# Matmul operands moved: activation rows 320 columns apart, operands at multiples of 512 bytes, a smaller scratch for DMAs

## What is computed

```
mod = silu(c) @ w_ada + b_ada                      # 2048 -> 6 * 2048, per sequence
h   = rmsnorm(x, norm1_g) * (1 + scale1) + shift1
qa, ka, va, qb, kb, vb, r, glr = split(h @ w_in)   # 2048 -> 6160
oa  = dilated window attention(qa, ka, va)         # samples also read 1024 cached rows each
ob  = gated linear attention(qb, kb, vb, gate(glr))
x   = x + gate1 * (concat(norm(oa), norm(ob) * silu(r)) @ w_out)        # 2048 -> 2048
h2  = rmsnorm(x, norm2_g) * (1 + scale2) + shift2
g, u = split(h2 @ w_up)                            # 2048 -> 2 * 5632
x   = x + gate2 * ((silu(causal_conv3(g)) * u) @ w_down)                # 5632 -> 2048
```

## The kernel before

| tensor | start before | above a multiple of 512 | start after | above a multiple of 512 |
|---|---|---|---|---|
| `ring` | 16512 | 128 | 8320 | 128 |
| `v_parts` | 26752 | 128 | 18560 | 128 |
| `kdm` | 126080 | 128 | 117888 | 128 |
| `ghi` | 153568 | 480 | 145376 | 480 |
| `hhi` | 159712 | 480 | 151552 | 0 |
| `hlo` | 178144 | 480 | 172032 | 0 |
| `whi` | 196576 | 480 | 192512 | 0 |
| `wlo` | 212960 | 480 | 208896 | 0 |
| `vals` | 159712 | 480 | 151552 | 0 |
| `kcT` | 200672 | 480 | 192512 | 0 |

## Time and profile before

### The profile page before, as it was taken

One profiled execution on the slowest core, in us unless ns is written; L12 is line 12 of the kernel. 1 busy time (PEld: TensorE's weight loads), 2 busy tenths in 40 slices (PEclk: granted clock), 3 DMA queues, 4 the chain that ended last, 5 costly groups with the idle time before them and its releaser, 6 DMA issues.

```text
span 1667.9 us, 29469 instructions
## 1 busy us (share of the span) xinstructions
PE 1624.7 (97%) x12258; PEld 1457.8 (87%) x12258; DVE 891.6 (53%) x1562; ACT 719.6 (43%) x1026; POOL 75.5 (5%) x132
## 2 busy tenths in 40 slices
PE   8999999999999889999999999999999999999997
PEld 4778888888888545998999999999999999999996
DVE  3555555455665453645654554545545465656563
ACT  3332444444555434534443333333334345545552
POOL 2000000000111000000000000000000000000000
PEclk8999999999999999999999999999999999999998
DMA  9998777778878999765845445554455446555450
GB/s 335 375 376 312 256 248 246 268 266 274 281 263 274 333 378 331 242 227 178 285 148 163 153 155 178 169 162 154 158 178 173 154 137 191 164 173 177 152 188 15
DMA packets 276113, 370.71 MB, mean 222 GB/s; under 512 B 8273, under 2 KB 192947, under 8 KB 275977
## 3 DMA queue, kind: packets, MB, share of 16 engines
q1 hardware_dynamic: 232928, 279.88, 50.6%
q10 hardware_dynamic: 35970, 71.45, 12.1%
q0 software_dynamic: 7088, 17.54, 3.2%
HBM read 358.96 MB, written 9.88 MB: 221 GB/s over the span
## 4 chain that ended last, share of the span: by engine, by line
PE 84%; issue 5%; DVE 4%; DMA 3%; ACT 2%; SPq 1%; POOL 0%; ACTq 0%; DVEq 0%; POOLq 0%
PE ps L920 23%; PE ps L921 22%; PE ps L922 22%; PE ps L871 4%; PE ps L1167 2%; DMA ring<-in_w_in 1%; PE ps L1182 1%; DMA vals<-in_w_ada 1%; PE ps L1212 1%; SPq L524 1%; DMA proj<-in_w_ada 1%; PE ps L878 1%; DVE wlo L1994 1%; ACT whi L1469 0%; PE ps L865 0%
## 5 line engine op out<-in xcount | busy, mean ns | idle before, releaser
L920 PE MATMUL ps<-hhi,whi 128*128 128x288 f32 x3136 | 939.8, 300 | 1.4 <-DVE hlo L1986 0.7
L922 PE MATMUL ps<-hhi,wlo 128*128 128x288 f32 x3136 | 924.5, 295 | 0.0
L921 PE MATMUL ps<-hlo,whi 128*128 128x288 f32 x3136 | 924.1, 295 | 0.0
L920 PEld LDWEIGHTS ps<-hhi,whi 128*128 128x128 f32 x3136 | 588.8, 188 | 40.0 <-issue 34.2
L921 PEld LDWEIGHTS ps<-hlo,whi 128*128 128x128 f32 x3136 | 588.4, 188 | 0.9
L922 PEld LDWEIGHTS ps<-hhi,wlo 128*128 128x128 f32 x3136 | 588.8, 188 | 0.0
L1855 DVE TENSOR_TENSOR wlo<-ring,whi 128x1024 fp32r<-128x1024 f32 x178 | 212.2, 1222 | 88.0 <-ACT whi L1452 87.5
L1452 ACT ACTIVATE whi<-ring 128x1024 fp32r<-128x1024 f32 x178 | 184.6, 1057 | 159.2 <-PE ps L922 159.2
L1994 DVE TENSOR_TENSOR wlo<-ring,whi 128x1024 fp32r<-128x1024 f32 x96 | 117.3, 1224 | 124.3 <-ACT whi L1469 124.1
L1469 ACT ACTIVATE whi<-ring 128x1024 fp32r<-128x1024 f32 x96 | 100.9, 1053 | 139.0 <-PE ps L922 113.9
L2483 DVE TENSOR_TENSOR wlo<-ring,whi 128x1024 fp32r<-128x1024 f32 (+1 forms) x94 | 105.7, 1131 | 57.3 <-ACT whi L1777 57.3
(11 more groups left out here) (312 smaller groups left out, 1189.2 us busy)
## 6 DMA issues: line engine op xcount, KB each, us to landing
ring<-in_w_up SPq DMA_DIRECT2D x88, 1024.0 KB, 5.1
ring<-in_w_ada ACTq DMA_DIRECT2D x58, 1024.0 KB, 8.5
ring<-in_w_in SPq DMA_DIRECT2D x48, 1024.0 KB, 9.1
ring<-in_w_down SPq DMA_DIRECT2D x32, 1408.0 KB, 6.7
ring<-in_cache_k_win SPq DMA_DIRECT2D x16, 1024.0 KB, 9.6
vals<-in_cache_v_win SPq DMA_DIRECT2D x32, 512.0 KB, 8.0
ring<-in_w_out SPq DMA_DIRECT2D x16, 1024.0 KB, 5.9
proj<-in_w_ada SPq DMA_DIRECT2D x14, 1024.0 KB, 10.7
```

The costliest lines, as they stand in the source:

```text
L920: mm(out, w_hi, x_hi, start=start, stop=False)
L921: mm(out, w_hi, x_lo, start=False, stop=False)
L922: return mm(out, w_lo, x_hi, start=False, stop=stop)
```

## The change

Three edits. The rows of `hhi` and `hlo` are put 320 columns apart (1280 bytes), of which the first 288 are used; every slice that the program takes of them is unchanged. `ln_first`, a small tensor that lay behind all others, moves ahead of `hhi` and is 8 columns wide (32 bytes), which shifts the four tensors so that each begins at a multiple of 512 bytes. The scratch for GpSimd's DMAs goes from 16384 to 8192 bytes in each partition, and everything behind it moves down by 8192 bytes. After it even rows of `hhi` and `hlo` begin at a multiple of 512, odd rows 256 above one, all stationary slices of `whi` and `wlo` at a multiple of 512.

```diff
@@ -18,6 +18,7 @@
 TOK = SEQ + NS
+ROW = 320
 PAST = 1024
@@ -170,9 +171,10 @@
         mrow = sb("mrow", [P, 512])
 
 
+        ln_first = sb("ln_first", [P, 8])[:, 0:1]
         with ExitStack() as parts:
-            hhi = sbr("hhi", [P, KD, TOK], parts)
-            hlo = sbr("hlo", [P, KD, TOK], parts)
+            hhi = sbr("hhi", [P, KD, ROW], parts)[:, :, 0:TOK]
+            hlo = sbr("hlo", [P, KD, ROW], parts)[:, :, 0:TOK]
             whi = sbr("whi", [P, BUFS, CHUNK], parts)
             wlo = sbr("wlo", [P, BUFS, CHUNK], parts)
@@ -212,7 +214,6 @@
         stat = work[:, 2016:2032]
-        ln_first = sb("ln_first", [P, 1])[:, :]
@@ -2523,7 +2524,7 @@
-    nc = bacc.Bacc("TRN2", target_bir_lowering=False, num_devices=1)
+    nc = bacc.Bacc("TRN2", target_bir_lowering=False, num_devices=1, dynamic_dma_scratch_size=8192)
```

## The result

The changed kernel takes 1655.91 us (median of 4 runs, 1654.88 to 1659.8), the kernel before beside it 1668.39 us (4 runs, 1666.74 to 1670.78): a ratio of 0.9925, with a 95% interval of 0.9913 to 0.9937. That is 12.5 us less; the forecast was 1657.5 us, 11.3 us less. A later set of 5 runs on another occasion gave 1655.67 against 1669.14 us, ratio 0.9917 (0.9904 to 0.9931). The ratios in this document are taken from all runs, and differ by up to 0.0006 from the quotient of the two medians.

What follows compares the result with a forecast made beforehand. TensorE's float32r matmul stream was taken to bound the kernel: 1667.9 - 11.3 from the step, all else 0, gave 1656.6 us profiled, 1657.5 as median. Own range 1651 to 1664; 8 in 10, 1603 to 1683.

Steps and rivals of the forecast that it cites:

- The bound: TensorE's 9408 float32r matmuls of 288 columns fill three quarters of the span; a nanosecond per step is worth 9.4 us.
- The term of the step: In those 9408 matmuls, rows beginning like the weights over 256 bytes take 131.7 ns, not 132.9: 11.3 us less; chance 0.35.
- rows 5 and 6: TensorE timelines in two loop orders: means 132.9 and 132.7 ns; even rows 2.5 ns quicker than odd only in the first.
- Rival 1: The matmul step does not depend on where operands start: no change, 1668.8 us; chance 0.28.
- rows 8: Timeline of `v_parts` and `kdm`, both 128 above a multiple of 512: 256 columns take 120 ns, 0.469 ns a column.
- It is not the length of the weight load.: Claim that the 12.9 ns of each step beyond the 120.0 ns pass does not come from loading the weights.
- Rows 7: Timeline of `gate_rank`, loading 16 columns instead of 128 with the same rows streamed: 131.9 ns a step, 1.0 ns less.
- Rival 2: Rows are fetched in 64-byte pieces, one wasted; 18 instead of 19 gives 125.9 ns, 66 us less, 1603 us; chance 0.14.
- Rival 3: Weight load and stream beginning at the same place hold each other up: 12.2 us more, 1681 us; chance 0.23.
- Rows written in runs of 288: VectorE and ScalarE instructions writing four runs instead of one of 1152 columns: counted 0, bound 13 us on VectorE.
- The scratch: Halved scratch for GpSimd's DMA queue: counted 0, bound 24.3 us more if a wait came again on TensorE's path.
- `vals` and `kcT`: Their moved starts matter from 550 to 660 us, where DMAs are full: counted 0, bounds 5.5 us either way.

Runs made afterwards that it cites:

- the starts alone: Changed kernel with rows 1152 bytes apart again (ROW 288), the four tensors still begun at multiples of 512: 1665.89 us, ratio 0.9978 to the kernel before, step 132.79 ns.
- the weights moved: Changed kernel with whi and wlo begun 128 bytes higher: 1670.11 us against 1669.50 for the kernel before, ratio 1.0008, step 133.34 ns.
- the 15 blocks moved together: In a kernel without the layer that only streams float32r matmuls, row and weights shifted together to 15 places from 32 to 480 bytes: 131.67 ns in all.
- The blocks: Kernels without the layer, streaming float32r matmuls at many starts, lengths and stationary widths; with weights at 0, rows at multiples of 32 gave 131.67 or about 133.33 ns.
- `steps`: First kernel without the layer, streaming 48 float32r matmuls a block at varied starts, row lengths and layouts; 256 columns with starts at 0 took 120.0 ns.
- the scratch alone: Kernel before with only GpSimd's DMA scratch halved to 8192 bytes: 1668.36 us against 1669.92, ratio 0.9995, step 132.80 ns.
- rows alone: Changed kernel with the four tensors begun 480 bytes above a multiple of 512 again, rows still 1280 apart: 1657.79 us, ratio 0.9933 to the kernel before, step 131.66 ns.
- rows 96 above: Changed kernel with rows begun 96 bytes above a multiple of 256, weights at a multiple of 256: 1662.84 us, ratio 0.9962 to the kernel before, step 132.15 ns.

## Why the prediction was right, point by point

- **The bound.** One nanosecond of the step is 9.4 us, and no other engine takes over. The steps 133.34, 131.66 and 130.04 ns gave 1670.11, 1655.91 and 1646.23 us: the first difference is worth 15.8 us by the step and gave 14.2, the second 15.2 and gave 9.7. So the bound holds for the loss and for the forecast; of the further gain a third did not reach the median.
- **The term of the step.** Forecast 132.9 to 131.7, 11.3 us; measured 132.80 to 131.66, 10.7 us. The reason, equal starts over 256 bytes, is borne out by the starts alone (no gain), the weights moved (a loss) and the 15 blocks moved together. It is not the whole rule. Other distances are as quick or quicker, one has two levels at the same addresses, and equal starts off the multiples of 32 are not alike. Equal starts were a quick place, not the quickest. Why the step depends on the starts at all no run shows.
- **Luck.** The median fell by 12.5 us where 11.3 were forecast. That this is so near is in part chance: the step gave 0.6 us less than forecast, and the shorter DRAIN, which the sum did not have, stands beside it with up to 2.8 us. Also, the 131.7 ns was the reading of even rows that alternate with odd ones; that a stream of even rows alone would keep it was assumed, and turned out so.
- **The reading of rows 5 and 6.** I took the difference of even and odd rows in one loop order for the effect, and the lack of one in the other order as an open doubt. The blocks go most of the way. With the starts of before, the loop order with the tile outside streams at 133.33 ns with no pattern of rows, and the other at 132.78; equal starts give 131.67 in both. In the kernel before, where the first chunks of `w_in` have the tile outside, the mean from 100 to 200 us is 133.08 ns, in short stretches. So the equal means of rows 5 and 6 did not speak against an effect of the starts. Rival 1 read the same rows as no effect and fell with them.
- **`v_parts` as evidence for rival 1.** It had equal starts already, 128 and 128, and its step was compared per column with the rows' step. That was the mistake in the comparison: what stands above columns / 2.4 is no share of the length, 13.3 ns at 256 columns and 11.7 at 288, so a row of 256 must look dearer per column. In the stream of `steps` 256 columns take 120.0 ns at equal starts, which is what rows 8 showed. No block has 256 columns at other starts.
- **"It is not the length of the weight load."** Rows 7 could not carry this, for the 16 columns of `ghi` also begin at other places from slice to slice. With starts fixed, the blocks of 288 columns give 133.33, 131.1, 130.0, 133.33 and 131.67 ns for 16, 32, 64, 96 and 128 stationary columns, in no order; at 256 columns a load of 32 instead of 128 saves 6.7 ns, at 512 it costs 5.0. The number of stationary columns does matter, and not as a shorter load would.
- **Rival 2** (pieces of 64 bytes) is refuted by the starts alone. **Rival 3** was right that the start of one operand relative to the other counts, and had the sign wrong. It priced the loss at 12.2 us over the kernel before; the weights moved by 128 cost 14.2 us over the changed kernel, which is no more than the gain taken back.
- **Two rules of pages.** By the Trainium skill's lines of 16 bytes ("SBUF — State Buffer", Specifications) no start in multiples of 32 should matter; the runs disagree, with 131.67 and 133.33 ns for starts that differ by 32. The Trainium skill's gap of N / 2.4 + 2.5 ns ("TensorE: Matmul & The Clock Gate", Back-to-back issue gap), which that section gives for a matmul by itself and the prediction took for a stream, is 122.5 for 288 columns; no placement of float32r came below 130.0.
- **Rows written in runs of 288.** Counted as 0, and it is: VectorE's 56 instructions of L2397 (L2398 after) take 61.6 us before and after, those of four rows 1358 ns each. The bound of 13 us had left out the 16 instructions of three rows, 1056 ns each, which would have added 5 us by the same working.
- **The scratch.** Counted as 0, with a loss as the bound. GpSimd's wait for the previous state is 25.1 us in three where it was 24.3, and TensorE waits for nothing of it; but the last DRAIN is 2.8 us shorter in the profiles. The timed runs with the scratch alone show -0.8 us, from -2.3 to 0.7, so in the time the 2.8 us are not established.
- **`vals` and `kcT`.** Bounds of 5.5 us either way. The stretch from the 4000th to the 4600th matmul took 80.3 us before and 79.2 after. It does not go with the placement: with the scratch alone it took 81.3, in the changed kernel with a scratch of 4096 bytes 80.2, and with rows alone, where `vals` and `kcT` begin 480 above a multiple of 512 as before, 79.3. So no effect is shown, and this stretch and the DRAIN are where the profile of the starts alone has most of its 4.3 us. What made that kernel 0.22% quicker is open.
- **The range.** 1657.5 with 5.5 us on either side is 1652 to 1663, not 1651 to 1664. Nothing hangs on it.

## What to carry to other kernels

In a stream of float32r matmuls bound by TensorE, the placement of the two operands in on-chip memory moved the step by about 5% with no instruction changed (130.0 to 136.6 ns at 288 columns). So it should be measured early, in one kernel that streams blocks at many placements, and then tried in the real order of the work. Rows of 1152 bytes, no multiple of 256, walked through good and bad placements; a padded row fixed one, and a slice a few columns in chose which. Read the step from start to start, and measure it at several lengths before any comparison per column. When a gain in the step does not reach the time, look for a stretch in which the granted clock fell.

## What was not expected of the hardware

- The step of 288 columns takes levels: 130.0, 131.67, 133.33 ns, which at 1.2 GHz would be 156, 158 and 160 periods, and means between them. One kernel ran the same matmuls at the same addresses at two of these levels by turns (rows 96 above).
- Starts that differ by 4 bytes matter: 130.0 ns at 28, 135.5 at 24, 133.33 at 20 bytes above the weights.
- The last DRAIN of GpSimd took 7.18 us with a scratch of 16384 bytes, 4.40 with 8192 and 4.40 with 4096. In the kernel of the blocks, with the scratch of 16384 and no DMA on GpSimd's queue, it took 0.04 us.
- A plain float32 matmul of 288 columns shows as two records 242.5 ns apart in the blocks, so 485 ns for the shape that float32r streams in 131.67.
- With 32 stationary columns instead of 128, 256 columns take 113.3 ns instead of 120.0, and 512 take 231.7 instead of 226.7.
